# Attention by head pairs in a two-block transformer kernel: sum and maximum in one VectorE instruction, the causal mask as a matmul, projections cut in halves around the scores, finished rows fetched from another queue

## The chip, the cores and the metric

The kernel runs on one core of a Trainium2 chip. The time is the device time of one launch in microseconds. Three runs of the kernel before gave a median of 3226.95 us (3218.61 to 3236.28). The granted clock of TensorE is written as a share of its full speed.

## What is computed

Two model blocks follow each other on 1024 tokens of width 1024, all in float32. Each holds mixers between a wide input projection and an output projection. Three of the mixers are softmax attention, and they are what the change touches or borders on:

```python
# sparse attention (dsa): 6 heads of 64; each query sees its 256 best keys, with a bias by distance
logits = einsum('bqhd,bqkhd->bhqk', qb, kg) * (dh ** -0.5)
logits = logits + moveaxis(bias, -1, 1)          # rb[t5_bucket(rel)]; beyond some 128 tokens it is rb[31]
p = softmax(where(rel >= 0, logits, -1e30))
# forgetting attention (fox): 16 heads of 64, causal, c = cumsum(log_sigmoid(f))
s = einsum('bqhd,bkhd->bhqk', qi, k) * scale
s = s + ci[..., None] - ck[:, :, None, :]
pr = softmax(where(kpos <= qpos, s, -inf))
# dilated window attention (dil): 8 heads of 128 in three patterns
```

A softmax does not change when a number is added to a whole row. The term `ci` and the far bias `rb[31]` are such numbers.

## The kernel before

**Split products.** Every wide projection is made of three fp32r matmuls per 128x128 weight tile, high part by high, high by low, low by high (lines 820 to 822). A half projection, the unit in which the program is ordered, is one 128-column weight block by 512 tokens: 8 times 3 matmuls of 128x512 into one PSUM bank (`half_T`). `half_X` is a half too, but only four transposes, of the projected values. GpSimd splits each weight block into its two parts (lines 693 and 695), SyncE loads it.

**Stages of the kernel.** After norm, first projections and the key selection come 3 passes of sparse attention (500 to 710 us of the span), the output projection, 8 passes of forgetting attention (884 to 1584), output and gate, 8 passes of dilated attention (to about 3000), output, gate and final norm.

**A pass of pair attention** (`pair_attention`, on each engine) treats two heads of 64 at once, in 8 steps of 128 queries; step i sees (i+1)*128 keys, in chunks of at most 512, so that steps 4 to 7 have two chunks. VectorE adds the decay (fox) or the selection mask and the far bias (dsa) to the scores in PSUM (lines 2188 and 2192), adds the causal block or the near bias (line 2206), and takes the negated row maximum (line 2211), each for both heads. ScalarE takes the exponential in place (line 1723). TensorE transposes the probabilities (line 1106), ScalarE copies them back (line 1733), TensorE multiplies them with the values (line 1121) and spreads the reciprocals (line 1132). `sread`, `mx`, `edone`, `tdone`, `te` are the semaphores between them. VectorE and ScalarE run one step ahead of TensorE.

**The order on TensorE in a step** is written out by hand: transposes of chunk 0, spread of the step before, then `part1` of the next pair's projection, second score chunk of step i+1, values of chunk 0, transposes of chunk 1, `part2`, values of chunk 1, first score chunk of step i+2. `proj_units` deals the 10 halves of "TTTTX" over the 8 fox steps: one each, but two in step 3 and two in step 7, and those of step 7 are the transposes. In the sparse passes `SPARSE_UNITS` gives a half to steps 0, 2, 4, 6 and 7 only. The last pass of each kind has no projection beside it, apart from the turning of the residual in the sparse one and the first output block in step 7.

**Finished rows.** What attention has made goes to DRAM (`y_scratch`), one 512 KB row block a pass. In the last pass ScalarE loads six of them back, and after step 1 a seventh (`load_rows`, line 1659), copies each to its high part (line 1665), and GpSimd makes the low part (line 700). In the dilated stage ScalarE also issues, ahead of these, the load of the 4 MB residual (line 1798).

Of the kernel before, what the change touches and what calls it, by code (L numbers as in the profile page):

```python
# [15 lines left out]
P = 128  # L16
# [12 lines left out]
TOPK = 256  # L29
IDX_H, IDX_D = 4, 32  # L30
# [109 lines left out]
ORDER = dict(dsa="TTTTX", fox="TTTTX", dil="TTTTTTTTXTXTX")  # L140
PAIR_ROLES = (("q", 0), ("k", 0), ("vT", 0), ("g", 0), ("v", 0))
# [64 lines left out]
SPARSE_UNITS = {0: 0, 2: 1, 4: 2, 6: 3, 7: 4}  # L206
# [25 lines left out]
def beside_pair(kind, p, t):  # L232

    if kind == "dsa":
        n = SPARSE_UNITS.get(t)
        return ([] if n is None else [((5 * p + n) // 2, (5 * p + n) % 2, None)]), []
    return proj_units(kind, t)


# [12 lines left out]
def host_constants():  # L252
# [5 lines left out]
    out["c_ones"] = np.ones((P, P), np.float32)  # L258
    out["c_diag"] = np.where(q >= np.arange(P)[None, :], 0.0, NEG).astype(np.float32)
# [32 lines left out]
def build(nc, a):  # L292
    ctx = ExitStack()
    with ctx:
# [90 lines left out]
        h_flat = hT[:, :, :].rearrange("p k t -> p (k t)")  # L385
        F = Area(h_flat, 0, KB * T)
# [73 lines left out]
        ccol = FX.take(16 * NT).rearrange("p (t h) -> p t h", h=16)  # L460
# [54 lines left out]
        SPLIT = sems("act_split", "in late hi lo")  # L515
# [20 lines left out]
        FC = sems("foxc", "x lsig cum sent t ev")  # L536
# [4 lines left out]
        dil_in = sem("dil_constants")  # L541

# [3 lines left out]
        def load_gain(eng, m):  # L546
# [7 lines left out]
        def _(sp):  # L554
# [79 lines left out]

            def up_and_gate(m):
                for j in range(4):
                    out_block(m, j)
# [179 lines left out]
        def _(pe):  # L817
# [245 lines left out]
            def pair_attention(kind, base, first):  # L1063
# [7 lines left out]
                def project(p, units):  # L1071
                    for b, half, _ in units:
# [4 lines left out]
                        else:  # L1077
                            half_T(n, c, n % 2, half)

                def one(p, turn_, follow):  # L1080
                    Q = sets[kind][set_of(kind, p)]

                    def scores(i, c):
# [3 lines left out]
                        wait_pass(pe, S["sread"], before + p, C, starts[i] + c)  # L1087
# [64 lines left out]
                    for i in range(NT):  # L1152
                        part1, part2 = beside_pair(kind, p, i)
# [3 lines left out]
                        if follow:  # L1157
                            project(next_pair(kind, p), part1)
# [1435 lines left out]
```

## Time and profile before

| | |
|---|---|
| runs | 3218.61, 3226.95, 3236.28 us |
| profiled execution | 3224.9 us, its span 3223.1 us |
| PE busy | 2927.1 us (91%) |
| DVE, ACT, POOL busy | 1326.9, 903.2, 1033.6 us |
| mean granted clock | 0.954 |
| chain that ended last | PE 77%, DVE 13%, ACT 5% |

The profile names engines PE (TensorE), PEld (its weight loads), DVE (VectorE), ACT (ScalarE), POOL (GpSimd), SP (SyncE). In a timeline row a bracket gives the idle time before the instruction and what ended it. A row of the waits gives the engine and line that waited, what it waited for, the total in us, how often, and the longest.

### The profile page before, as it was taken

The page shows a single profiled execution, that of the slowest core. Times are in us where ns is not written, and L with a number is a line of the kernel's source. Part 1 is how long each engine was busy: PE and PEld are TensorE (multiplying, and loading weights), DVE is VectorE, ACT ScalarE, POOL GpSimd, SP SyncE. Part 2 cuts the span into 40 slices and gives each one's busy share as a digit, 9 for nine tenths or more (in the row PEclk, how much of TensorE's full clock was granted, in tenths as well). Part 3 has the DMA queues.
Part 4 walks back from the last instruction along what each step waited for, and adds up shares of the span by engine and source line. Part 5 has one row for each costly group of instructions (what it writes and reads, how often), then busy time and mean ns, then how long its engine had stood idle before and what let it go on. Part 6 is the DMA issues. An engine that isn't in the chain of part 4 may idle for free.

```text
span 3223.1 us, 39797 instructions
## 1 busy us (share of the span) xinstructions
PE 2927.1 (91%) x16484; PEld 2229.9 (69%) x16484; DVE 1326.9 (41%) x2447; ACT 903.2 (28%) x1689; POOL 1033.6 (32%) x447
## 2 busy tenths in 40 slices
PE   6979887879899998898899899999999999997998
PEld 4746674557666666665688677777777777775786
DVE  7999986555544444444634301111111111113322
ACT  4322313352233333333311322222222222223112
POOL 2613371124221212122353233342232323242541
PEclk8979899989999999999899999999999999998999
DMA  4100021031111111111122111111111111113211
GB/s 98 33 20 27 20 62 51 9 105 41 47 40 46 46 40 40 46 40 44 59 68 72 48 44 40 40 40 40 40 45 34 46 40 40 40 40 125 59 46 59
DMA packets 222223, 154.96 MB, mean 48 GB/s; under 512 B 26278, under 2 KB 208972, under 8 KB 221916
## 3 DMA queue, kind: packets, MB, share of 16 engines
q1 hardware_dynamic: 206908, 107.34, 11.9%
q10 hardware_dynamic: 15136, 45.08, 3.8%
q8 instruction: 131, 2.15, 0.3%
q14 instruction: 48, 0.39, 0.0%
HBM read 132.93 MB, written 19.47 MB: 47 GB/s over the span
## 4 chain that ended last, share of the span: by engine, by line
PE 77%; DVE 13%; ACT 5%; issue 3%; POOL 1%; DMA 1%; ACTq 0%; DVEq 0%; POOLq 0%
PE proj L820 20%; PE proj L821 19%; PE proj L822 19%; ACT arena L1723 3%; PE score L1106 2%; PE score L1092 2%; DVE arena L2154 2%; DVE arena L2152 2%; DVE arena L2206 2%; PE out L1121 2%; PE score L1235 1%; PE out L1288 1%; DVE arena L2289 1%; DVE arena L2211 1%; PE score L1244 1%
## 5 line engine op out<-in xcount | busy, mean ns | idle before, releaser
L820 PE MATMUL proj<-act_hi,w_hi 128*128 128x512 f32 x2592 | 1052.8, 406 | 46.7 <-POOL w_lo L695 28.3
L821 PE MATMUL proj<-act_lo,w_hi 128*128 128x512 f32 x2592 | 1025.4, 396 | 0.0
L822 PE MATMUL proj<-act_hi,w_lo 128*128 128x512 f32 x2592 | 1024.3, 395 | 0.0
L693 POOL TENSOR_TENSOR w_hi<-w_raw,ones 128x1024 fp32r<-128x1024 f32 x181 | 432.3, 2388 | 1844.2 <-PE proj L822 1827.3
L820 PEld LDWEIGHTS proj<-act_hi,w_hi 128*128 128x128 f32 x2592 | 496.8, 192 | 177.0 <-issue 33.6
L822 PEld LDWEIGHTS proj<-act_hi,w_lo 128*128 128x128 f32 x2592 | 496.2, 191 | 107.9
L821 PEld LDWEIGHTS proj<-act_lo,w_hi 128*128 128x128 f32 x2592 | 497.6, 192 | 99.6 <-issue 0.2
L695 POOL TENSOR_TENSOR w_lo<-w_raw,w_hi 128x1024 fp32r<-128x1024 f32 x181 | 448.9, 2480 | 14.2
L1707 ACT ACTIVATE arena<-proj 128x512 f32<-128x512 f32 x236 | 175.3, 752 | 922.5 <-PE proj L822 898.9
L2342 DVE SCALAR_TENSOR_TENSOR arena<-out,arena 128x128 f32<-128x128 f32 x64 | 17.9, 288 | 610.4 <-PE out L1254 610.4
L2188 DVE SCALAR_TENSOR_TENSOR arena<-score,arena 128x512 f32<-128x512 f32 (+2 forms) x192 | 109.6, 613 | 344.7 <-PE score L1092 344.7
L1106 PE MATMUL score<-ident,arena 128*128 128x128 f32 x792 | 141.2, 307 | 65.4 <-ACT arena L1723 63.5
L1106 PEld LDWEIGHTS score<-ident,arena 128*128 128x128 f32 x792 | 92.8, 151 | 146.8 <-ACT arena L1723 132.4
L2289 DVE SCALAR_TENSOR_TENSOR arena<-arena,score 128x256 f32<-128x256 f32 (+1 forms) x192 | 76.6, 427 | 264.1 <-PE score L1235 210.4
L2152 DVE MAX8 arena<-arena 128x8 f32<-128x384 f32 (+5 forms) x192 | 171.6, 894 | 5.9
L1723 ACT ACTIVATE arena<-arena 128x256 f32<-128x256 f32 (+7 forms) x176 | 134.9, 769 | 128.2 <-DVE arena L2211 128.2
L2154 DVE MATCH_REPLACE8 arena<-arena 128x384 f32<-128x384 f32 (+5 forms) x192 | 168.5, 878 | 0.0
L1733 ACT ACTIVATE arena<-score 128x512 f32<-128x512 f32 (+3 forms) x264 | 119.4, 487 | 115.1 <-PE score L1106 113.1
L1707 ACT ACTIVATE hT<-proj 128x512 f32<-128x512 f32 x78 | 65.7, 850 | 273.2 <-PE proj L822 258.1
L1121 PE MATMUL out<-arena 128*64 128x128 f32 x1296 | 102.3, 295 | 29.4 <-ACT arena L1733 29.4
L2211 DVE TENSOR_REDUCE arena<-arena 128x1 f32<-128x256 f32 (+7 forms) x176 | 123.5, 742 | 0.0
L1121 PEld LDWEIGHTS out<-arena 128*64 128x64 f32 x1296 | 74.9, 145 | 65.8 <-ACT arena L1733 40.3
(244 smaller groups left out, 3058.1 us busy)
## 6 DMA issues: line engine op xcount, KB each, us to landing
w_raw<-dil_w_in_dram SPq DMA_DIRECT2D x80, 512.0 KB, 3.7
w_raw<-fox_w_in_dram SPq DMA_DIRECT2D x32, 512.0 KB, 4.0
w_raw<-w_in_dram SPq DMA_DIRECT2D x23, 512.0 KB, 3.8
y_scratch<-arena ACTq DMA_DIRECT2D x21, 512.0 KB, 3.7
act_lo<-y_scratch ACTq DMA_DIRECT2D x21, 512.0 KB, 8.1
arena<-decay_scratch ACTq DMA_DIRECT2D x16, 512.0 KB, 5.3
w_raw<-ple_w_gate_dram SPq DMA_DIRECT2D x16, 512.0 KB, 3.8
arena<-x_dram SPq DMA_DIRECT2D x12, 512.0 KB, 4.1
```

What stands on the lines that cost most here:

```text
L693: pool.tensor_tensor(hi, raw, one.unsqueeze(1).broadcast_to([P, KB, P]), ALU.mult).then_inc(w_hi_done, 1)
L695: pool.tensor_tensor(lo, raw, hi.bitcast(F32), ALU.subtract).then_inc(w_split, 1)
L820: pe.matmul(bank, hi, a_hi, start=first, stop=False)
L821: pe.matmul(bank, hi, a_lo, start=False, stop=False)
L822: return pe.matmul(bank, lo, a_hi, start=False, stop=last)
L1106: mm = pe.transpose(score[:, 1, hh * 512 + b * P:hh * 512 + (b + 1) * P], R["p"][hh][i % 2][:, (b0 + b) * P:(b0 + b + 1) * P], ident[:, :])
L1121: mm = pe.matmul(obanks[i % 2][cols, 0:P], Q["v"][0][:, b0 + b, cols], R["pT"][hh][:, q % 2, b * P:(b + 1) * P], start=(b0 + b == 0), stop ...
L1707: act.activation(dst, src, ACT.Copy, scale=scale if role == "q" else 1.0).then_inc(pass_free[half], 1)
L1723: act.activation(R["p"][hh][i % 2][:, 0:width], R["p"][hh][i % 2][:, 0:width], ACT.Exp, bias=R["st"][:, s:s + 1], accum_out=R["st"][:, 16 ...
L2152: dve.max(top8, scores[:, 0:w]).then_inc(IX["top"], 1)
L2154: dve.match_replace(scores[:, 0:w], top8, scores[:, 0:w], -3e38).then_inc(IX["top"], 1)
L2211: dve.tensor_reduce(R["st"][:, s:s + 1], R["p"][hh][i % 2][:, 0:width], AX.X, ALU.max, negate=True)\
```

## The change

1. VectorE: in fox a single instruction (`tensor_tensor_reduce`) adds decay and scores, negates, and keeps a running minimum; the per-query decay `ccol`, its transposes and its copy are gone, and so are the block add and the maximum. In dsa the far part of a row is made by the same instruction, the last 256 columns by a plain add out of PSUM and then one such instruction with the bias table; `rb31` is gone. The exponential gets `scale=-1.0`.
2. TensorE: in fox the last 128 columns of a row get the causal block by a bf16 matmul of identity and block, one per head, accumulated on the scores. `diag` is reloaded for it as packed bf16.
3. `pair_units` replaces `proj_units` and `SPARSE_UNITS`; "TTTTX" becomes "TTTXT". In fox each step has one full half, cut in two parts of 12 matmuls, of which the first stands ahead of the second score chunk and the second after the transposes of chunk 1. In the sparse passes each step has one such part.
4. SyncE loads the finished rows, in `up_and_gate` and beside the residual loads, ahead of the weights that follow, and the 4 MB residual after them. ScalarE waits per two rows (`in0`, `in1`, `in2`).

```diff
-ORDER = dict(dsa="TTTTX", fox="TTTTX", dil="TTTTTTTTXTXTX")
+ORDER = dict(dsa="TTTXT", fox="TTTXT", dil="TTTTTTTTXTXTX")
+PAIR_HALVES = ((0, 0), (0, 1), (1, 0), (1, 1), (2, 0), (2, 1), (3, 0), (4, 0), (3, 1), (4, 1))
+def pair_units(kind, p, t):
+    def unit(n, part=None):
+        return (n // 2, n % 2, part)
+    if kind == "fox":
+        n = t if t < 6 else t + 2
+        return ([unit(7)] if t == 6 else []), unit(n, 0), unit(n, 1), ([unit(6)] if t == 5 else [])
+    if p == 0:
+        return [], unit(t // 2, t % 2), None, []
+    n = 4 + t // 2 if t < 4 else 6 + t // 2
+    return ([unit(7)] if t == 4 else []), unit(n, t % 2), None, ([unit(6)] if t == 3 else [])
...
+        def scores_read(eng, kind, p, q):
+            S, before = AT[kind], PAIRS_BEFORE[kind]
+            chunks = chunks_of(attention_steps(kind))
+            starts = chunk_starts(chunks)
+            if kind == "dsa":
+                wait_pass(eng, S["sread"], before + p, starts[-1], q)
+                return
+            i = max([0] + [i for i in range(NT) if starts[i + 1] <= q])
+            if q == 0 or starts[i + 1] == q:
+                eng.wait_ge(S["mx"], 2 * NT * (before + p) + (2 * (i + 1) if q else 0))
+            else:
+                partial = [q_ for q_ in range(1, q + 1) if q_ not in starts]
+                eng.wait_ge(fox_read, p * (starts[-1] - NT) + len(partial))
...
+            def finished_rows(kind, base):
+                m = MIXER[kind]
+                for half in range(2):
+                    sp.wait_ge(pass_done[half], base + PASSES[kind] * len(ORDER[kind]))
+                sp.wait_ge(AT[kind]["ysent"], 16 * (STORES_BEFORE[kind] + PASSES[kind] - 2))
+                for j, k in enumerate(rows_before(m)[:6]):
+                    sp.dma_start(act_lo[:, k].bitcast(F32), yd[k * P:(k + 1) * P, :]).then_inc(SPLIT[f"in{j // 2}"], 16)
+            def late_row(kind):
+                k = rows_before(MIXER[kind])[6]
+                sp.wait_ge(AT[kind]["ysent"], 16 * (STORES_BEFORE[kind] + PASSES[kind] - 1))
+                sp.dma_start(act_lo[:, k].bitcast(F32), yd[k * P:(k + 1) * P, :]).then_inc(SPLIT["late"], 16)
...
+                if m == 1:
+                    finished_rows("fox", C_FOX)
+                    late_row("fox")
+                else:
+                    finished_rows("dil", C_DIL)
+                    late_row("dil")
+                    sp.wait_ge(AT["dil"]["sdone"], 2 * NT * (PASSES["dil"] - 1) + 1)
+                    sp.dma_start(hT[:, :, :], xd).then_inc(xback, 16)
...
+            sp.wait_ge(IX["sel"], 9)
+            sp.dma_start(diag[:, :].bitcast(I32), a["c_diag_half"]).then_inc(halved, 16)
...
+                    if t == 2:
+                        sp.wait_ge(GL["ysent"], 16 * 5)
+                        finished_rows("dsa", C_DSA)
+                        late_row("dsa")
                     sp.wait_ge(N0["raw"], 2 * (t - 2) + 2)
...
                             mm = pe.matmul(score[:, 0, hh * 512:hh * 512 + w], Q["q"][0][rows, i * P:(i + 1) * P],
-                                           Q["k"][0][rows, lo:lo + w], start=True, stop=True)
+                                           Q["k"][0][rows, lo:lo + w], start=True, stop=not causal(i, lo, w),
+                                           skip_group_check=causal(i, lo, w))
+                        if causal(i, lo, w):
+                            for hh in range(2):
+                                end = hh * 512 + w
+                                mm = pe.matmul(score[:, 0, end - P:end], diag_half[:, 0], diag_half[:, 1], start=False, stop=True,
+                                               skip_group_check=True)
                         mm.then_inc(S["sdone"], 1)
...
-                            act.activation(R["p"][hh][i % 2][:, 0:width], R["p"][hh][i % 2][:, 0:width], ACT.Exp,
-                                           bias=R["st"][:, s:s + 1], accum_out=R["st"][:, 16 + s:17 + s]).then_inc(S["edone"], 1)
+                            act.activation(R["p"][hh][i % 2][:, 0:width], R["p"][hh][i % 2][:, 0:width], ACT.Exp,
+                                           bias=R["st"][:, s:s + 1], scale=-1.0, accum_out=R["st"][:, 16 + s:17 + s]).then_inc(S["edone"], 1)
...
-                    if not follow:
-                        load_rows(kind, True, base)
...
+                                if kind == "fox":
+                                    ins = dve.tensor_tensor_reduce(row[:, lo:lo + w], cB[turn_][hh][:, lo:lo + w], src, -1.0,
+                                                                   most if c else LARGE, ALU.add, ALU.min, most)
+                                at = mask_offset(i) + lo
+                                if far:
+                                    ins = dve.tensor_tensor_reduce(row[:, lo:lo + far], maskb[:, at:at + far], src[:, 0:far], -1.0,
+                                                                   most if c else LARGE, ALU.add, ALU.min, most)
+                                if far < w:
+                                    ins = dve.tensor_tensor(row[:, lo + far:lo + w], src[:, far:w], maskb[:, at + far:at + w], ALU.add)
+                        if kind == "dsa":
+                                dve.tensor_tensor_reduce(row[:, near:width], row[:, near:width], tbias[:, 2 * p + hh, 2 * P - width + near:2 * P],
+                                                         -1.0, most if near else LARGE, ALU.add, ALU.min, most).then_inc(S["mx"], 1)
-                            dve.tensor_tensor(row[:, width - w:width], row[:, width - w:width], near, ALU.add)\
-                               .then_inc(S["pre"], 1)
-                            dve.tensor_reduce(R["st"][:, s:s + 1], R["p"][hh][i % 2][:, 0:width], AX.X, ALU.max, negate=True)\
-                               .then_inc(S["mx"], 1)
```

## Rows read from the trace of the kernel before

**Rows 1.** By stage: length, busy PE, PEld, DVE, ACT, POOL, then granted clock, DMA.
```profile
500.00:647.00 147.00, 124.26 (x788) 82.02 (x786) 76.56 (x157) 54.93 (x124) 18.92 (x8) 0.93 0.05 19
647.00:710.00 63.00, 47.83 (x331) 30.96 (x330) 44.70 (x95) 37.40 (x78) 16.70 (x7) 0.86 0.38 134
884.00:1519.00 635.00, 578.68 (x3434) 407.89 (x3436) 276.28 (x565) 210.02 (x467) 136.67 (x57) 0.96 0.14 41
1519.00:1584.00 65.00, 50.21 (x332) 30.70 (x329) 41.95 (x95) 31.19 (x65) 16.50 (x7) 0.81 0.18 65
```
**Rows 2.** Waits of PE in the fox passes 0 to 6 (884 to 1519).
```profile
PE score L1106 <- ACT arena L1723: 36.6, 37, 3.3
PE out L1121 <- ACT arena L1733: 12.9, 27, 0.6
PE score L1092 <- DVE arena L2188: 5.7, 7, 0.8
```
**Rows 3.** Waits of PE in sparse passes 0 and 1 (500 to 647).
```profile
PE score L1106 <- ACT arena L1723: 16.4, 18, 3.5
PE score L1092 <- DVE arena L2192: 10.4, 4, 9.2
PE out L1121 <- ACT arena L1733: 4.7, 8, 0.7
```
**Rows 4.** Timeline of a fox pass around its step 7.
```profile
1142.61 1.41 DVE L2188 SCALAR_TENSOR_TENSOR arena<-score,arena 128x512 f32<-128x512 f32 x2 [7.22 <-PE score L1092]
...
1144.03 2.35 POOL L695 TENSOR_TENSOR w_lo<-w_raw,w_hi 128x1024 fp32r<-128x1024 f32 x1
1144.05 2.67 DVE L2206 TENSOR_TENSOR arena<-arena,diag 128x128 f32<-128x128 f32 x2
...
1146.65 2.33 DVE L2211 TENSOR_REDUCE arena<-arena 128x1 f32<-128x1024 f32 x2
1147.89 1.15 ACT L1723 ACTIVATE arena<-arena 128x1024 f32<-128x1024 f32 x1 [2.91 <-DVE arena L2211]
...
1149.18 2.25 PE L1106 MATMUL score<-ident,arena 128*128 128x128 f32 x8 [3.27 <-ACT arena L1723]
```
**Rows 5.** Timeline of PE at a change between projection and attention, and eight transposes.
```profile
1064.15 1.09 PE L1106 MATMUL score<-ident,arena 128*128 128x128 f32 x8
...
1075.40 0.39 PE L822 MATMUL proj<-act_hi,w_lo 128*128 128x512 f32 x1
1075.71 0.44 PE L1121 MATMUL out<-arena 128*64 128x128 f32 x4
...
1078.18 0.50 PE L820 MATMUL proj<-act_hi,w_hi 128*128 128x512 f32 x1
1078.52 0.40 PE L821 MATMUL proj<-act_lo,w_hi 128*128 128x512 f32 x1
1078.76 0.39 PE L822 MATMUL proj<-act_hi,w_lo 128*128 128x512 f32 x1
```
**Rows 6.** Timeline of the last fox pass: row loads, then values.
```profile
1526.21 3.56 ACTq L1659 DMA_DIRECT2D act_lo<-y_scratch  x6
...
1531.32 0.70 PE L1121 MATMUL out<-arena 128*64 128x128 f32 x4 [5.35 <-ACT arena L1733]
```
**Rows 7.** Timeline of the last dilated pass.
```profile
2946.41 1.08 PE L1288 MATMUL out<-arena 128*32 128x128 f32 x16 [4.50 <-ACT arena L1790]
...
2961.89 2.00 ACT L1665 ACTIVATE act_hi<-act_lo 128x1024 fp32r<-128x1024 f32 x2 [9.87 <-DMA act_lo<-y_scratch]
...
2964.43 1.08 PE L1288 MATMUL out<-arena 128*32 128x128 f32 x16 [6.79 <-ACT arena L1790]
```
**Rows 8.** VectorE's groups of instructions, whole span.
```profile
L2154 DVE MATCH_VALUE_LOAD arena<-arena 128x8 f32 x192 | 17.7, 92 | 6.6
L2251 DVE SCALAR_TENSOR_TENSOR arena<-arena 128x1024 f32<-128x1024 f32 x9 | 11.0, 1227 | 12.5 <-ACT arena L1752 12.4
L2045 DVE TENSOR_TENSOR_SCAN arena<-arena 128x1024 f32<-128x1024 f32 x2 | 6.1, 3093 | 0.0
```

More of the change, by code:

```diff
@@ L1 @@
 from contextlib import ExitStack
+from itertools import product
 import math
@@ L205, with units_done @@
 RESIDUAL_TURNS = ((0,), (1,), (2,), (3,), (4,), (5,), (6, 7), ())
-SPARSE_UNITS = {0: 0, 2: 1, 4: 2, 6: 3, 7: 4}
+PAIR_HALVES = ((0, 0), (0, 1), (1, 0), (1, 1), (2, 0), (2, 1), (3, 0), (4, 0), (3, 1), (4, 1))
[9 more added lines that the diff above has]
+    return ([unit(7)] if t == 4 else []), unit(n, t % 2), None, ([unit(6)] if t == 3 else [])
+def units_done(units):
+    return [u for u in units if u is not None and u[2] != 0]
 def pass_beside(n):
@@ L258, in host_constants @@
     out["c_ones"] = np.ones((P, P), np.float32)
+    halves = np.concatenate([np.eye(P, dtype=np.float32), np.where(q >= np.arange(P)[None, :], 0.0, NEG).astype(np.float32)], axis=1)
+    out["c_diag_half"] = np.ascontiguousarray(halves.view(np.uint32) >> 16).astype(np.uint16).view(np.int32)
     out["c_diag"] = np.where(q >= np.arange(P)[None, :], 0.0, NEG).astype(np.float32)
@@ L1071, in project @@
                 def project(p, units):
-                    for b, half, _ in units:
+                    for b, half, part in units:
                         n = p * NW + base + weight_of(order, b)
@@ L1077, in project, with causal @@
                         else:
-                            half_T(n, c, n % 2, half)
+                            half_T(n, c, n % 2, half, part)
+                def causal(i, lo, w):
+                    return kind == "fox" and lo + w == (i + 1) * P
                 def one(p, turn_, follow):
@@ L1086, in scores @@
                             return
[L1087 removed]
+                        scores_read(pe, kind, p, starts[i] + c)
                         lo = 512 * c
@@ L1176, in one @@
                         scores(i + 2, 0)
+                        if follow:
+                            project(next_pair(kind, p), tail)
                     if not follow:
                         spread(NT - 1)
-                halves = [(b, half, None) for b in range(NB) for half in range(2)]
+                halves = [(b, half, None) for b, half in PAIR_HALVES]
                 if kind == "dsa":
@@ L1342, in attention @@
                 out_last(m, kind)
-            def forget_columns():
-                pe.wait_ge(FC["cum"], 1)
-                for t in range(NT):
-                    mm = pe.transpose(obank[:, t * 16:t * 16 + 16], crow[0:16, t * P:(t + 1) * P], ident[0:16, 0:16])
-                mm.then_inc(FC["t"], 1)
-                pe.wait_ge(FC["ev"], 1)
-                later(pe, NF, "back", 2 * KB)
             def turn_p(m, b):
@@ L1649, in _ @@
                 gla_step(n)
-            def load_rows(kind, first, base):
-                m = MIXER[kind]
-                if kind == "dsa" and first:
-                    act.wait_ge(GL["ysent"], 16 * 5)
-                act.wait_ge(AT[kind]["ysent"], 16 * (STORES_BEFORE[kind] + PASSES[kind] - (2 if first else 1)))
-                for half in range(2):
-                    act.wait_ge(pass_done[half], base + PASSES[kind] * len(ORDER[kind]))
-                for k in rows_before(m)[:6] if first else rows_before(m)[6:]:
-                    act.dma_start(act_lo[:, k].bitcast(F32), yd[k * P:(k + 1) * P, :]).then_inc(SPLIT["in" if first else "late"], 16)
             def split_rows(m, i):
@@ L1826, in attention @@
                         projected(0, 0, [(0, half, None), (1, half, None)])
-                halves = [(b, half, None) for b in range(NB) for half in range(2)]
+                halves = [(b, half, None) for b, half in (PAIR_HALVES if kind != "dil" else product(range(NB), range(2)))]
                 if kind == "dsa":
```

85 lines of the change are left out of this document (37 added, 48 removed).

## The prediction

> **What bounds the kernel now.** I read the page first: PE is busy for 91% of the span and makes 77% of the chain that ended last. So an edit pays where PE stands still or runs at a low clock, or where it takes work off PE; what it takes off VectorE (41% busy) pays only through that. The table by stage then says where PE stands still [rows 1]. The fox passes 0 to 6 last 635 us with PE busy 578.7, at a mean clock of 0.96; the last fox pass has 14.8 us without PE in 65; the sparse passes have 22.7 in 147 and, the last, 15.2 in 63. Everything else in the kernel is outside the change, but for the last dilated pass. The waits say for whom PE stood: in fox 55.2 us (36.6 + 12.9 + 5.7), nearly all for the exponential or for ScalarE's copy [rows 2]. In the two sparse passes it is 31.5 us, of which one wait of 9.2 us is the end of the key selection, which the change leaves: 22.3 us are in play [rows 3]. The timeline of step 7 shows what stands behind "waits for the exponential" [rows 4]: scores are read by two adds in 1.41 us, then come the block adds (2.67 us for two of 128 columns, while GpSimd's product runs, longer than two of 512 columns out of PSUM), the two maxima (2.33 us), and the exponential begins 5.3 us after the first add. PE has only transposed values as cover there and waits 3.27 us. After that wait the eight transposes take 2.25 us, against 1.09 us elsewhere [rows 5]; part of that is the second head's wait, part the clock. Of the two levels, 1.2 and 2.4 GHz, a mean of 0.96 over 635 us is 51 us at the lower one.
>
> **VectorE, fox.** Removed per step: two block adds and two maxima; the adds stay as the new instruction. In step 7 the exponential could start after one add and its accumulation, some 0.8 us after the scores, in place of 5.3. No row has the new instruction. Below: the same time as the old one, 0.70 us for 512 columns [rows 4]. Above: the rate of the running scan, 3093 ns for 1024 columns [rows 8], which is 1.5 us for 512. I take the old time plus 0.1 us, as the small second instruction that match-replace brings costs 92 ns [rows 8], since one source and one result are as before. VectorE is not on the path of the fox passes at either end: between the second score chunk and the next read of PE on the same bank lie 5.8 us of PE work (values 1.1, transposes 0.9, the second part of the half 2.9, values 0.9).
>
> **The cuts, fox.** Each step now has a full half, and half of it lies between the score chunk and the transposes that wait for it. Chunk-1 scores to the exponentials' end is then 0.1 + 1.6 + 2.6, about 4.3 us, beside 5.8 of PE work plus the next scores. ScalarE has the copy of chunk 1 (1.1 us) ahead of the exponential in its queue, and it still fits. What stays is the start of a pass, where the scores of step 1 wait for row 0 and nothing covers it: 1.5 to 2 us a pass. So of 55.2 us 14 stay and **41 go**. The long waits being gone, I give back **14 us of clock**, from nothing to 25 (half of the 51).
>
> **What PE gets in return.** The mask: 8 steps of 8 passes with 2 matmuls, 128 in all. Nearest row: eight float32 transposes of 128 columns in 1.09 us, 7 steps of 0.117 us [rows 5]. 128 by 0.117 is **15 us lost**; below 0, should they hide in the gaps; above, unpipelined, the 0.27 us of one transpose and 0.14 of its weight load, 52 us. The cuts: within a half the starts follow each other by 0.24 us (1078.52 to 1078.76); on leaving it the next start comes after 0.31 (1075.40 to 1075.71), on coming back the second comes after 0.34 (1078.18 to 1078.52) [rows 5]; 0.2 us a cut, 56 cuts in fox and 8 in the sparse passes, **13 us lost**, from nothing to 0.5 us each, 32. The transposes of `ccol` and the wait for their copy save 1 us.
>
> A rule of the Trainium skill puts the mask lower: TensorE: Matmul & The Clock Gate, section Back-to-back issue gap, gives 134 cycles for 128 columns, which would be 7 us for the 128. No run here shows a bf16 matmul in a stream, and the sum does not use it.
>
> **The last fox pass.** ScalarE issues six loads, 3.56 us on its queue, ahead of the gate and the first copy, and PE waits 5.35 us for that copy [rows 6]. With SyncE issuing them the gate's 1.1 us and the copy stay: 3.8 us gained. In the six later steps the exponential now waits for ScalarE's own copy of chunk 1 rather than the maximum, so a step gains some 1 us, not the whole block add and maximum: 6 us. Two adds no longer collide with GpSimd: 2 us. Together **12**.
>
> **The sparse passes.** The far part is covered as in fox, but the last 256 columns need a plain add and a second pass, so a wide row gets only some 0.8 us shorter; the collision with GpSimd stays, since both sources of the bias instruction are in SBUF. What helps is that each step has a part as cover, in place of five steps in eight. ScalarE's queue (copy, then exponential) leaves some 1.2 us a wide step, 5 us a pass. 22.3 less 10 is **12**, with **3 of clock**. The last pass gains the same 3.8 from the row loads and some 4 from the rows: **8**. There SyncE has seven row loads ahead of the residual's third tile; that tile is needed two steps into the pass, so I price it at nothing; if its cover fails, it is one load, 4 us, in one step.
>
> **The last dilated pass.** PE waits 4.50 us for the copy behind ScalarE's issues and 6.79 us behind ScalarE's wait of 9.87 us for a row that lands after the 4 MB residual [rows 7]. SyncE starts the rows when the projections end, ahead of the pass's first exponential, and puts the residual behind them; the copies to the high parts (2.0 us) move forward. **10 of 11.3**. VectorE wants the residual only after the pass, so it is late for nobody. SyncE's weight loads behind these waits are split by GpSimd only after the seven rows, so they hide too.
>
> **Sum.** 41 + 14 + 1 + 12 + 12 + 3 + 8 + 10 = 101 gained, 15 + 13 = 28 lost, 73 us net. Against the profiled execution, 3224.9 us (its span 3223.1), that is 3152; the median of the runs shown lies 2 us above it, so 3154 us.
>
> **Rivals.**
> 1. *The waits only move.* ScalarE's queue or the score bank ends the step in place of VectorE. For it: ScalarE has copies, exponentials and evacuation in a fixed order. Against: it is busy for 210 us in 635 [rows 1]. If half of the fox and sparse gains (41, 12, 14, 3) stay away, 35 us, the time is 3189. Chance 0.17.
> 2. *The clock stays up and mask and cuts hide.* 11 more of clock, 28 not lost: 3115. Chance 0.1.
> 3. *Slower: the new instruction has a large fixed cost.* Four passes lack cover to take it: the three sparse ones with 32 each and the last fox one with 24, 120 in all, of which two thirds are on the path. At f us each this is 80 f, and it eats the 73 us at f of 0.9; past 1.1 it is slower by 0.5%. At 1.5 us it is 3274. The one small second instruction among its rows takes 92 ns [rows 8]. Chance 0.04.
> 4. *Two float32 sources in SBUF at half the rate.* For the 48 bias instructions of the sparse passes: 256 columns, 0.27 us each, 13 us on VectorE, 9 on the path: 3163. The row against: two sources in SBUF, 1024 columns in 1227 ns [rows 8], full rate, but without accumulation. Chance 0.12. This is a point of the Trainium skill, Vector Engine (DVE) Microarchitecture Reference, section Points that are easy to get wrong, which says that such an instruction halves its throughput because no port is left for the accumulator; by that rule, the row of the plain instruction disagrees, and whether the new one follows it no run here shows.
> 5. *The change does not do what it says*: the mask's unpipelined price, 37 us more, takes back what the cover brings: 3191. Chance 0.05.
>
> **How the numbers follow.** The forecast itself has 0.52, with an own range of 3135 to 3173. The range reaches up to rivals 1 and 5 and down to rival 2: 3115 to 3192, leaving out rival 3 and tails, some 0.18. This kernel's measurement tells some 0.5%, 16 us, from no change; faster by more is all below 3211, so all but rival 3 and the tail of 1 and 5. Faster 0.92, within 0.5% 0.04, slower 0.04.
>
> **What would show it.** In the new profile a fox pass should last some 86 us instead of 90.7 (635 by 7), PE's waits for the exponential there fall to a fifth, the clock of the stage rise to 0.98 or more; the new VectorE instruction should take some 0.7 us in the mean, a mask matmul add 0.1 us to a step; no wait over 2 us should stand behind ScalarE at the start of the three last passes. I am wrong if new waits of PE stand at the scores behind VectorE, if the new instruction takes over 1.5 us for 512 columns, or if PE's busy time in fox rises by more than 35 us.

## The result and the profile after

| | before | after |
|---|---|---|
| median (runs) | 3225.99 us (3218.61 to 3236.28, 4) | 3126.37 us (3119.94 to 3129.75, 4) |
| profiled execution, span | 3224.9, 3223.1 us | 3124.53, 3122.7 us |
| PE, DVE, ACT, POOL busy | 2927.1, 1326.9, 903.2, 1033.6 us | 2899.4, 1137.8, 895.2, 1031.9 us |
| granted clock | 0.954 | 0.966 |

The ratio is 0.9679, with a 95% interval of 0.9660 to 0.9698: the changed kernel is faster by some 100 us. The forecast was 3154 us, inside a range of 3115 to 3192, and 73 us of gain.

The windows of the changed kernel, cut where its stages begin and end, answer to [rows 1]: sparse passes 0 and 1, the last sparse pass, fox passes 0 to 6, the last fox pass, and the last dilated pass.

```profile
502.00:632.00 130.00, 117.20 (x788) 78.41 (x788) 57.79 (x213) 52.89 (x124) 18.20 (x8) 0.97 0.09 30
632.00:678.00 46.00, 39.66 (x316) 25.38 (x313) 31.74 (x117) 34.59 (x75) 15.06 (x7) 0.96 0.47 161
856.00:1438.00 582.00, 570.61 (x3582) 399.72 (x3582) 131.65 (x509) 207.77 (x470) 132.99 (x57) 0.99 0.15 43
1438.00:1478.00 40.00, 33.19 (x272) 19.28 (x270) 21.40 (x83) 27.99 (x61) 17.82 (x8) 0.96 0.40 131
2844.00:2894.00 50.00, 32.72 (x378) 21.53 (x367) 30.40 (x68) 19.60 (x35) 15.79 (x7) 0.83 0.50 186
```

In fox, VectorE's busy time has halved (276.28 us [rows 1], now 131.65) and PE stands still for 11 us in 582.

For the difference to close, each stage is cut at an instruction that both kernels have (an attention stage begins with its first score matmul, the sparse one with the scores of its step 1, and a last pass ends at the first matmul of the output projection in its step 7) and its length is split in three from the trace: time in which PE has no matmul; time in which it works while the record of the granted clock stands at the lower level, of which half is lost, since that level is half the other; and the rest, its work at full clock. All in us, "idle" and "low" being the first two:

| stage | before: length, idle, low | after: length, idle, low | gained |
|---|---|---|---|
| sparse passes 0, 1 | 146.9, 22.7, 20.1 | 129.2, 12.3, 6.6 | 17.7 |
| last sparse pass | 59.6, 15.2, 11.9 | 46.7, 6.3, 3.4 | 12.9 |
| fox passes 0 to 6 | 639.4, 56.8, 44.6 | 582.1, 11.4, 6.8 | 57.3 |
| last fox pass | 53.9, 14.5, 17.6 | 40.2, 6.8, 3.4 | 13.7 |
| dilated passes 0 to 6 | 1018.2, 39.8, 6.1 | 1025.4, 40.6, 19.8 | -7.2 |
| last dilated pass | 58.0, 24.2, 15.9 | 50.0, 17.3, 14.0 | 8.0 |
| all else | 1247.1, 122.8, 105.6 | 1249.1, 128.6, 97.2 | -2.0 |
| sum | 3223.1, 296.0, 221.8 | 3122.7, 223.3, 151.2 | 100.4 |

So 72.7 us came from idle time, 35.3 from the clock (half of 70.6), and 7.6 were paid in work, which is what is left of the 100.4. The 7 us lost in the dilated passes are the lower level, in code that the change does not touch: its share there lay anywhere between 6 and 24 us over the kernels run below, and at 6.3 in e8, which has all of the change. Of the 2 us in "all else", 3 are real, at the start (last section).

The waits of PE, fox passes 0 to 6, answer to [rows 2]:

```profile
PE score L1158 <- DVE arena L2240: 5.8, 7, 1.1
PE out L1193 <- ACT arena L1790: 5.6, 6, 1.7
PE score L1158 <- ACT arena L1764: 0.9, 1, 0.9
```

55.2 us have become 12.3. No wait for an exponential is left; every wait that stays lies within the first 10 us or so of a pass. In the sparse passes, answering to [rows 3], the 9.1 us are the end of the key selection again:

```profile
PE score L1158 <- DVE arena L2252: 9.7, 2, 9.1
PE score L1178 <- ACT arena L1780: 7.0, 8, 1.8
PE out L1193 <- ACT arena L1790: 4.7, 8, 0.7
```

The timeline of a fox pass around step 7 answers to [rows 4] (the rows of weight loads and projections are left out):

```profile
1338.38 1.13 PE L1158 MATMUL score<-arena 64*128 64x512 f32 x4
1339.44 0.29 PE L1164 MATMUL score<-diag 128*128 128x128 bf16 x2
1339.65 1.10 PE L1193 MATMUL out<-arena 128*64 128x128 f32 x16
1339.76 0.75 DVE L2240 CUSTOM_DVE_ANT_0 arena<-arena,score 128x512 f32<-128x512 f32 x1 [5.03 <-PE score L1164]
1340.43 0.08 DVE L2240 DVE_READ_ACCUMULATOR2_ANT arena<- 128x1 f32 x1
...
1341.27 0.87 ACT L1790 ACTIVATE arena<-score 128x384 f32<-128x384 f32 x2 [4.94 <-PE score L1178]
...
1342.02 1.15 ACT L1780 ACTIVATE arena<-arena 128x1024 f32<-128x1024 f32 x1
...
1345.03 1.09 PE L1178 MATMUL score<-ident,arena 128*128 128x128 f32 x8
```

The new instruction shows as two, the sum and the read of its accumulator. After 0.8 us the first head is ready; the exponential starts 2.3 us after the first sum, no longer held by VectorE but by ScalarE's own copy. The transposes follow with no wait and take 1.09 us. VectorE's groups by form:

```profile
L2240 DVE CUSTOM_DVE_ANT_0 arena<-arena,score 128x512 f32<-128x512 f32 x96 | 63.2, 696 | 225.0 <-PE score L1158 140.0 <-PE score L1164 85.0
L2260 DVE CUSTOM_DVE_ANT_0 arena<-arena 128x256 f32<-128x256 f32 x42 | 28.6, 718 | 0.7
L2240 DVE DVE_READ_ACCUMULATOR2_ANT arena<- 128x1 f32 x192 | 15.8, 83 | 0.0
L2240 DVE CUSTOM_DVE_ANT_0 arena<-arena,score 128x256 f32<-128x256 f32 x32 | 13.1, 447 | 28.7 <-PE score L1164 28.7
```

The starts of the last fox and last dilated pass answer to [rows 6, 7]:

```profile
1436.94 2.75 SPq L674 DMA_DIRECT2D act_lo<-y_scratch  x6
...
1443.12 0.44 PE L1193 MATMUL out<-arena 128*64 128x128 f32 x4 [2.21 <-ACT arena L1790]
```

```profile
2842.22 2.80 SPq L674 DMA_DIRECT2D act_lo<-y_scratch  x6
...
2850.58 0.79 PE L1364 MATMUL out<-arena 128*32 128x128 f32 x16
...
2854.91 1.99 ACT L1722 ACTIVATE act_hi<-act_lo 128x1024 fp32r<-128x1024 f32 x2
...
2855.38 0.32 SPq L680 DMA_DIRECT2D act_lo<-y_scratch  x1
2855.47 0.29 DVE L2391 SCALAR_TENSOR_TENSOR act_hi<-out,arena 128x128 fp32r<-128x128 f32 x1 [0.85 <-DMA y_scratch<-arena]
...
2855.75 0.43 SPq L692 DMA_DIRECT2D hT<-x_scratch  x1
2856.03 4.70 POOL L763 TENSOR_TENSOR act_lo<-act_lo,act_hi 128x1024 fp32r<-128x1024 f32 x2 [10.35 <-ACT act_hi L1722]
2856.06 2.47 DVE L2397 TENSOR_TENSOR act_lo<-arena,act_hi 128x128 fp32r<-128x128 f32 x1
...
2859.10 1.22 PE L1320 MATMUL score<-arena 128*128 128x256 f32 x2 [3.33 <-DVE arena L2340]
```

The six issues stand on SyncE. In fox the wait of 5.35 us is 2.21, in the dilated pass those of 4.50 and 6.79 us are gone. But there a new one has come: since the copies to the high parts are made earlier, GpSimd's products of the same rows now meet a small subtraction of VectorE (line 2397), which takes 2.47 us here, and PE waits 3.33 us for the scores that VectorE reads behind it. Its six instructions in this stage took 3.7 us before (one of them 2.19) and take 7.5 now. PE's waits for VectorE's additions to the scores, which stand in the same queue, first before (2936 to 2994), then after (2844 to 2894):

```profile
PE score L1244 <- DVE arena L2289: 7.9, 6, 3.0
```

```profile
PE score L1320 <- DVE arena L2340: 12.3, 6, 3.3
```

With the loads back on ScalarE (e7 below) they are 8.9 us.

### The profile page after: what moved, and what is told of

It is laid out like the page before. It is cut to its first block, busy times and chain, and to the rows that moved or that the text cites. A ratio compares the mean times of both kernels' runs of the same rounds, so it can differ in the third digit from the quotient of the medians.

```text
span 3122.7 us, 40092 instructions
## 1 busy us (share of the span) xinstructions
PE 2899.4 (93%) x16604; PEld 2208.9 (71%) x16604; DVE 1137.8 (36%) x2460; ACT 895.2 (29%) x1689; POOL 1031.9 (33%) x447
## 4 chain that ended last, share of the span: by engine, by line
PE 82%; DVE 9%; issue 3%; ACT 3%; DMA 1%; POOL 1%; ACTq 1%; DVEq 0%; POOLq 0%
PE proj L883 20%; PE proj L884 19%; PE proj L885 19%; PE score L1158 3%; PE out L1193 3%; PE score L1178 3%; DVE arena L2202 2%; DVE arena L2200 2%; PE score L1311 2%; DVE arena L2340 1%; PE out L1364 1%; PE score L1320 1%; PE out L1369 1%; PE out L1204 1%; PE out L883 1%
## 5 line engine op out<-in xcount | busy, mean ns | idle before, releaser
L2240 DVE CUSTOM_DVE_ANT_0 arena<-arena,score 128x512 f32<-128x512 f32 (+2 forms) x192 | 102.8, 572 | 428.2 <-PE score L1164 288.0
L1178 PE MATMUL score<-ident,arena 128*128 128x128 f32 x792 | 117.7, 283 | 9.6 <-ACT arena L1780 9.3
L1178 PEld LDWEIGHTS score<-ident,arena 128*128 128x128 f32 x792 | 85.2, 141 | 55.4 <-issue 30.0
L1158 PE MATMUL score<-arena 64*128 64x512 f32 (+3 forms) x432 | 99.8, 539 | 9.7 <-DVE arena L2240 7.3
L1193 PE MATMUL out<-arena 128*64 128x128 f32 x1296 | 95.9, 282 | 11.8 <-ACT arena L1790 11.8
L883 PE MATMUL proj<-res_parts,w_hi 128*128 128x512 f32 x256 | 101.5, 397 | 0.0
```

Of the source, the lines that this page charges most:

```text
L883: pe.matmul(bank, hi, a_hi, start=first, stop=False)
L1178: mm = pe.transpose(score[:, 1, hh * 512 + b * P:hh * 512 + (b + 1) * P], R["p"][hh][i % 2][:, (b0 + b) * P:(b0 + b + 1) * P], ident[:, :])
L1193: mm = pe.matmul(obanks[i % 2][cols, 0:P], Q["v"][0][:, b0 + b, cols], R["pT"][hh][:, q % 2, b * P:(b + 1) * P], start=(b0 + b == 0), stop ...
```

## The experiments

Runs sent together share a chip and the runs of the kernel before. Below, "changed" is the changed kernel, 3126.37 us (ratio 0.9679). The same kernel on another chip took 3122.95 us (e12, below), so differences of some 3 us between runs that were not sent together say nothing in the total; the stages of the trace are steadier (fox passes 0 to 6 last 582 us in both).

**What the mask costs.** The first run has no mask matmuls, so its rows are not causal; the second has three for each.

```diff
-                    return kind == "fox" and lo + w == (i + 1) * P
+                    return kind == "fox" and lo + w == (i + 1) * P and False
```

> The changed kernel without the 128 mask matmuls in the forgetting passes; it leaves out the causal block of a row, all else is as it was. If the price is the one of the forecast (0.117 us each, all of it on TensorE's path), it is 15 us faster than the changed kernel, 3111 us. If a mask matmul costs half of that, as a rival from the stage sum would have it (the stage shows mask and cuts together at some 9 us, where 24 were priced), it is 7 us faster, 3119 us. If the masks hide in waits, the time stays at 3126 us, and the waits of TensorE for VectorE and ScalarE in the stage (12 us) rise by what is taken away.

```diff
-                                mm = pe.matmul(score[:, 0, end - P:end], diag_half[:, 0], diag_half[:, 1], start=False, stop=True,
-                                               skip_group_check=True)
+                                for again in range(3):
+                                    mm = pe.matmul(score[:, 0, end - P:end], diag_half[:, 0], diag_half[:, 1], start=False, stop=again == 2,
+                                                   skip_group_check=True)
```

> The changed kernel with each mask matmul issued three times, 256 more of them; the mask only becomes more negative. Same theories, other side and twice the lever: 0.117 us each gives 30 us more, 3156 us; half of it 15 us more, 3141 us; hidden: 3126 us. If the three matmuls of one bank stand 0.06 us apart in the timeline, the stream price is the lower one and the rest is the price of the change of weights.

Measured: 3111.46 us (ratio 0.9643, 0.9622 to 0.9663) and 3140.5 us (0.9733, 0.9712 to 0.9755), 15 us less and 14 more than changed. Clock and idle time left aside, the work at full clock in the whole span is 10.9 us less and 13.7 more: 0.085 us for each of 128 and 0.054 for each of 256 further ones. The timelines agree. In the changed kernel a pair takes 0.21 us of PE's time (1339.44 to 1339.65 above); with three of each:

```profile
1401.18 0.34 PEld L1165 LDWEIGHTS score<-diag 128*128 128x128 bf16 x6
1401.18 0.51 PE L1165 MATMUL score<-diag 128*128 128x128 bf16 x6
1401.62 1.10 PE L1194 MATMUL out<-arena 128*64 128x128 f32 x16
```

0.44 us for six, so 0.23 for the four added. The forecast's 0.117 was too much, and a third (by the work) to a half (by the timeline) of what a mask matmul costs belongs to the change from float32 scores to the mask, not to the stream. The expectation of e1 (3111 us at 0.117 each) was met by its total, but 4 of its 15 us are clock and idle time.

The Trainium skill (TensorE: Matmul & The Clock Gate, section Back-to-back issue gap) has 134 cycles for 128 columns, 0.056 us at 2.4 GHz, as the gap of an isolated matmul. The same section of the Trainium skill puts the spacing in a stream of weight loads and matmuls at some 81 ns for 128 columns. The trace agrees with the first, though each of the six matmuls has a weight load of its own: 0.057 us.

**Where the half projection stands.** Both runs have 56 cuts fewer. The diff is that of the first (e3), the half ahead of the second score chunk; the second (e4) has `None, unit(n)` there, the half behind the transposes of chunk 1.

```diff
-        return ([unit(7)] if t == 6 else []), unit(n, 0), unit(n, 1), ([unit(6)] if t == 5 else [])
+        return ([unit(7)] if t == 6 else []), unit(n), None, ([unit(6)] if t == 5 else [])
```

> The changed kernel with the half projection of a fox step in one piece, ahead of the second score chunk (56 cuts gone, the second place empty). If a cut costs the forecast's 0.2 us and nothing needs its cover, it is 11 us faster, 3115 us. Main theory: the cover is needed. From the second score chunk to the transposes that wait for its exponential only values, transposes, values and the next scores are left, some 4.0 us of PE work against the 4.3 us of chain (scores read 1.6, exponentials 2.6), and the exponential stands behind a copy: 0.5 to 1 us of wait in four steps of each of seven passes, 14 to 28 us, so 3130 to 3145 us, with TensorE waiting for the exponential at the transposes in steps 4 to 7.

> The changed kernel with the half of a fox step in one piece behind the transposes of chunk 1 (56 cuts gone, the first place empty). If only the long cover matters (second score chunk to the next transposes), it is 11 us faster, 3115 us. Main theory: the values of chunk 0 then follow the transposes they need with nothing between but the spread in the steps without a second score chunk (0, 1, 2 and 7): ScalarE's copy takes some 1.4 us from the transposes' end, so about 1 us of wait in 28 steps, 28 us less the 11 us of cuts, 3143 us, with the waits standing at the values behind the copy.

Measured: 3139.65 us (0.9728, 0.9706 to 0.9751) and 3156.48 us (0.9779, 0.9756 to 0.9801). Fox passes 0 to 6 lasted 595.3 and 613.8 us in place of 582.1. PE's waits there, first with the half in the first place, then in the second:

```profile
PE out L1193 <- ACT arena L1790: 16.3, 28, 0.7
PE score L1158 <- DVE arena L2240: 5.8, 7, 1.1
PE score L1178 <- ACT arena L1780: 5.0, 14, 0.5
```

```profile
PE out L1193 <- ACT arena L1790: 27.3, 28, 3.7
PE score L1158 <- DVE arena L2240: 6.2, 8, 1.1
```

The sum of the first was right and its reason was not: most of the wait (16.3 us, 28 times) stands at the values, for ScalarE's copy, and only 5.0 at the exponential. For the second it is the other way round: 28 waits of a mean 1 us are as expected, but the sum (3143) was 13 us too low, since the lower clock came back with the waits (6.8 us at the lower level to 38.4, worth 15.8) and no term stood for it. So the cut halves serve two covers, one for the exponential and one for each copy.

**Each part alone.** e5 and e9 are the changed kernel with the old order; in e5 the order of the dilated heads was altered by mistake ("TTTTTTTTTXXTX"), so that only its sparse and fox stages count. e6 is the kernel before with the new order alone.

```diff
-ORDER = dict(dsa="TTTXT", fox="TTTXT", dil="TTTTTTTTXTXTX")
+ORDER = dict(dsa="TTTTX", fox="TTTTX", dil="TTTTTTTTXTXTX")
+SPARSE_UNITS = {0: 0, 2: 1, 4: 2, 6: 3, 7: 4}
+    part1, part2 = proj_units(kind, t)
```

> The changed kernel without its third part: the order TTTTX, whole halves, two of them in steps 3 and 7 of a forgetting pass, and a half in five of the eight sparse steps, as before; the new VectorE instruction, the mask matmuls and SyncE's row loads stay. Main theory, that order and shorter rows both were needed: the whole half ahead of the second score chunk cost 13 us, step 7 has only transposes as cover again (some 3 us in 7 passes), the sparse passes lose some 5, so 3126 + 13 + 20 + 5, some 3160 us with a clock again lower at the ends of the passes. Rival, that the VectorE part alone brought the gain: 3135 to 3145 us.

> The kernel before with the third part alone: order TTTXT, halves cut in two around the second score chunk, a part in each sparse step. VectorE's adds, block adds and maxima, its ccol and ScalarE's row loads are those of before. Main theory: the new place of the halves gives 7.8 us of cover behind the second score chunk, against a chain of 5.3 us to the exponential and 2.3 of exponentials, so that most of the 57 us without TensorE in the seven passes goes, but not all in steps in which GpSimd's product holds up the block add: some 30 us of wait and 10 of clock are gained, cuts cost 6, 3190 us. Rival: the row in VectorE is still too long, nothing is gained and the cuts cost: 3225 to 3235 us. Other rival: order alone does all of it: 3150 us.

> The changed kernel without its third part, once more, now with the order of the dilated heads as it is in both kernels (the run before had it altered). From the stages of that run: 10 us more than the changed kernel in the seven forgetting passes, 2.6 in the sparse ones, 1 in the last passes, and 3 less ahead of them: 3137 us. That is the gain of 89 us from the VectorE part, the mask and the row loads without the order. Rival, that the altered dilated order had hidden a loss elsewhere: 3150 us or more.

| fox passes 0 to 6 | total | length | idle | low | work |
|---|---|---|---|---|---|
| before | 3225.99 | 639.4 | 56.8 | 44.6 | 560.2 |
| e6, order alone | 3167.92 | 572.5 | 8.2 | 9.9 | 559.3 |
| e9, all but the order | 3131.53 | 590.5 | 24.1 | 0.0 | 566.5 |
| changed | 3126.37 | 582.1 | 11.4 | 6.8 | 567.2 |
| e11, below | 3105.28 | 568.9 | 7.8 | 3.0 | 559.5 |

e6 has a ratio of 0.9806 (0.9768 to 0.9844), e9 of 0.9713 (0.9687 to 0.9739); e5 was 3122.9 us, with 592.2 us in the fox passes. Alone, the order gains 56 us against the runs of the kernel before that were sent with it (63 by the ratio) and the other three parts some 91, together 100: they take away the same waits. The total of e9 does not stand clear of that of the changed kernel (3131.53 against 3126.37, intervals that overlap); its stages do, with 8.4 us more in fox passes 0 to 6 and 2.5 in the sparse passes. All three expectations missed on the same side: e5's 3160 and e6's 3190 assumed that both parts were needed. In fox passes 0 to 6 the order alone, with VectorE's long rows, is 9.6 us *faster* than the whole change, by 7.9 us of work, which is mostly the mask (without the mask matmuls the changed kernel has 557.9 in e1, 559.5 in e11). And e11, which has the order and the new instruction without the mask matmuls, is only 3.6 us better there than the order alone: once each step has its cover, the shorter rows are worth little in these passes. Where the cover is smaller they are worth more: with ScalarE's loads in both, sparse passes 0 and 1 last 147.5 us in e6 and 129.1 in e7 (below), the last fox pass 52.5 and 44.6. In the sparse stages it is the rows that count and not the order: passes 0 and 1 last 146.9 us before, 147.5 with the order alone, 131.7 in e9, 129.2 in the changed kernel.

**The row loads.** ScalarE issues them (and the residual) again.

```diff
+                    if not follow:
+                        load_rows(kind, True, base)
...
-                    finished_rows("fox", C_FOX)
-                    late_row("fox")
```

> The changed kernel without its fourth part: ScalarE issues the row loads again (and the 4 MB residual in the dilated pass), SyncE does not. By the forecast it costs 3.8 us in the last sparse and 3.8 in the last forgetting pass and 10 in the last dilated one, 17.6 us and no clock: 3144 us. The stages of the changed kernel show 8.9, 7.7 and 6.9 us less without TensorE in these three passes and some 6 us of clock. If all of that belongs to the loads, it is 3156 us; if the shorter rows did the work and the loads hide, 3130 us.

Measured: 3142.6 us (0.9737, 0.9709 to 0.9765), 16 us more. The last sparse pass is 6.2 us longer, the last fox pass 4.4, the last dilated pass 5.0, together 15.6. The forecast of 17.6 was near.

**How much room VectorE has.**

```diff
+                                    dve.tensor_tensor(row[:, lo:lo + w], cB[turn_][hh][:, lo:lo + w], src, ALU.add).then_inc(twice, 1)
+                                    wait_pass(dve, twice, p, 2 * C, 2 * (starts[i] + c) + hh + 1)
```

> The changed kernel with a plain add of the same operands and shape ahead of each new VectorE instruction of the forgetting passes, and a wait for it: VectorE's time for a row doubles, some 13 us more in each of the eight passes, TensorE's work is as it was. Main theory, VectorE has slack of 1.5 us in a step that has a half as cover, and none at the start of a pass and in the last pass: 1 us in each of seven passes and some 9 in the last, 3142 us, with hardly a wait for the exponential in the middle of a pass. Rival, that VectorE's chain still sets the pace: two thirds of 8 times 13 us, 3195 us.

Measured: 3134.45 us (0.9716, 0.9687 to 0.9746). Fox passes 0 to 6 are 5.1 us longer, the last one 10.5 (6.6 of them idle, 4.2 clock). Seven waits for VectorE at the starts of passes (5.8 us, now 9.4) are all that is new in the middle passes:

```profile
PE score L1159 <- DVE arena L2243: 9.4, 7, 1.3
PE out L1194 <- ACT arena L1791: 6.0, 5, 2.0
PE score L1159 <- ACT arena L1765: 0.9, 1, 0.9
```

**The mask back on VectorE.** If VectorE has room and PE has none, the mask belongs to VectorE. e10 does so in passes 0 to 6, e11 in all eight, e12 is the changed kernel again, on the chip of e11.

```diff
+                                    if far < w:
+                                        ins = dve.tensor_tensor(row[:, lo + far:lo + w], src[:, far:w], cB[turn_][hh][:, lo + far:lo + w], ALU.add)
...
+                                dve.tensor_tensor_reduce(row[:, near:width], row[:, near:width], diag_half[:, 1],
+                                                         -1.0, most if near else LARGE, ALU.add, ALU.min, most).then_inc(S["mx"], 1)
```

> The changed kernel with the causal block added by VectorE in the seven forgetting passes that have projections beside them: the last 128 columns of a row by a plain add, then one new instruction with the block (bf16) as second source, as the sparse passes do it; the last pass keeps the mask matmuls. 112 of 128 mask matmuls go, at 0.085 us each 9.5 us. Main theory, VectorE has room there (with the order alone and the old, longer rows the seven passes lasted 572.5 us, against 582.1 in the changed kernel, with less time without TensorE): 3117 us, faster than the changed kernel. Rival: the block instruction has both sources in SBUF and stands beside GpSimd's products, and waits come back at the starts of passes and in single steps, 1 us or more a pass: 3126 us or above.

> As the run before (causal block by VectorE), now in the last forgetting pass too, so that no mask matmul is left. There TensorE has no projection as cover. TensorE loses 16 mask matmuls, 1.4 us; VectorE has two more instructions and an accumulator read for each head and step, 0.29 + 0.50 + 0.08 us less the 0.13 that the first instruction gets shorter, 0.74 us, 1.5 us a step, 12 us in the pass. The doubled adds put 10.5 us of some 13 on the path there. Main theory: the last pass is 7 to 9 us longer (40.6 to some 48), 3118 us. Rival, VectorE has room there too: 1 us shorter, 3109 us.

> The changed kernel again, beside the runs with the mask on VectorE, to compare them on one chip: 3126 us, 8 us slower than the run with all blocks on VectorE if the last pass loses 7 to 9 us there; its fox passes 0 to 6 last 582 us and those of the other 568.

Measured: e10 3110.74 us (0.9638, 0.9613 to 0.9664), e11 3105.28 us (0.9624, 0.9607 to 0.9641), e12 3122.95 us (0.9679, 0.9661 to 0.9698). On one chip e11 is 17.7 us faster than the changed kernel, and no run of the one reaches into the runs of the other (3103.96 to 3107.15, 3119.85 to 3128.56). Both are faster than their forecasts (3117 and 3118). In fox passes 0 to 6 the work falls by 7.7 us and the idle time by 3.6; with the last pass the stages that the edit touches give 11.5 us. The other 6 stand in the dilated passes, in code that both kernels share, and vary there from kernel to kernel as said above: that they come from the mask is not shown. The windows of e10 for these passes, against 570.61 us of busy PE in 582:

```profile
863.00:1431.00 568.00, 559.68 (x3468) 392.13 (x3468) 187.76 (x789) 210.36 (x471) 134.48 (x57) 1.00 0.15 44
```

VectorE is busy 56 us more, and PE waits for it no longer than in the changed kernel (seven times at the starts of passes, 4.8 us against 5.8). The last pass, where I had put 7 to 9 us, was 1.7 us longer than in e12 (42.0 against 40.3): its waits for the exponential are 2.0 us where they were 0.7.

## Why the prediction was right

The direction, the bound and the mechanism (long waits for the exponential go, and with them the time at the lower clock) held. The total came nearer than its terms did. The 27 us that the forecast lacked are made of three errors: costs booked at 28 us were 7.6 (20 too high), the clock booked at 17 gave 35.3 (18 too low), and waits booked at 84 gave 72.7 (11 too high), which the first two hide. In the last passes the clock had no term at all. And one attribution was wrong. By its own terms:

- **Waits in fox**, 41 of 55.2, 14 to stay: 42.9 went and 12.3 stayed, at the starts of passes as forecast (1.7 us a pass).
- **Clock in fox**, 14: 18.9 (half of 44.6 less 6.8). The bound of 25 was right; half of it was too cautious. In the record of the clock before, a stretch at the lower level begins at every end of a pass, as at 1148.2 us, where the wait of 3.27 us in [rows 4] falls, nine from 885 to 1514; after, two are left, at 857.5 and 1195.5 us, and in e4 they were back, seven of them, with the waits.
- **Mask**, 15 for 128: 10.9. The term was mis-sized by the nearest row: a transpose's 0.117 us for a stream that costs 0.054 and an entry that costs the rest.
- **Cuts**, 13 for 64: too high, and no single price came out. Without them the fox work is 4.1 us less in e3 and 8.6 in e4, 0.07 to 0.15 us a cut; but e6 has all the cuts and no more work than before (559.3 against 560.2), and e9 has none and saves 0.7. At most 0.15, perhaps nothing; which, stays open. Mask and cuts were booked at 28 us; the work of the span grew by 7.6.
- **ccol**, 1: not seen; the stage ahead of fox took 177.1 us and takes 177.4.
- **Last fox pass**, 12 less 2 of mask: 13.7, but by luck: 7.7 of it is idle time and 7.1 is clock, which was not booked. The loads are 4.4 of it (3.8 forecast), by e7.
- **Sparse passes 0 and 1**, 12 and 3 of clock: 10.4 of idle time and 6.8 of clock. The size held, the reason failed: "what helps is that each step has a part as cover". e6 has that cover and gains nothing there, e9 has not and gains 15.2 of 17.7: the shorter rows did it.
- **Last sparse pass**, 8: 12.9, of which 8.9 are idle time and 4.3 the clock. The loads are 6.2 of it, by e7.
- **Last dilated pass**, 10: 8.0, of which 6.9 are idle time. What failed there is a wait that had no term: the 11.3 us behind ScalarE are gone, but 4.4 have come back behind VectorE, by the subtraction that now meets GpSimd's products. With the loads back on ScalarE the stage is 55.0 us, 3.0 short of the 58.0 before; that ScalarE now waits for two rows at a time may be the reason, which was not run by itself, and with SyncE's loads the stage itself lay anywhere between 47.7 and 50.6 us.
- **The new instruction**, 0.8 us for 512 columns: 0.696 and 0.083.

**The rivals.** The waits did not merely move (1), apart from the 4.4 us in the last dilated pass. The clock stayed up (2), and its 3115 us was nearer than 3154 to what came, though mask and cuts did not hide: e1 and e2 show the masks paid in full. A fixed cost of the new instruction (3) is 0.083 us. Two float32 sources in SBUF at half rate (4): the bias instruction has a mean of 718 ns for 256 columns against 447 with a source in PSUM, which looks like the rule, 0.27 us more. But of all 48 bias instructions, 41 took 0.29 to 0.49 us, one 0.59, and six took 1.7 to 2.6; one of these six, in the timeline of the last sparse pass:

```profile
646.93 2.54 POOL L763 TENSOR_TENSOR act_lo<-act_lo,act_hi 128x1024 fp32r<-128x1024 f32 x1
647.19 2.57 DVE L2260 CUSTOM_DVE_ANT_0 arena<-arena 128x256 f32<-128x256 f32 x1
```

It is as long as GpSimd's product beside it. The seven that took more than 0.5 us are those that met such a product, so the mean comes from few collisions, not from a rate. The point of the Trainium skill (Vector Engine (DVE) Microarchitecture Reference, section Points that are easy to get wrong) is made there for another instruction, `S2S2D2_STT`. In this one it did not show: 0.48 us for 256 columns alone. Rival 5 is excluded by e1 and e2.

**The signs.** A fox pass lasts 83.1 us (86 forecast), the clock of the stage is 0.99, the new instruction takes 0.70 us. One sign failed: a wait of 2.21 us, over the 2 us allowed, still stands behind ScalarE at the start of the last fox pass.

What the prediction did not ask is whether each part was needed beside the others. It summed over one list of waits and gave all of it to the change as a whole, which is why the total held while the parts overlapped by half. The shorter rows, without the mask and the loads, were not run alone, so their share of e9's 91 us is open.

## What to carry to other kernels

Two edits that remove the same waits are not worth their sum; run each alone, since the second may keep only its cost. Here the mask matmul moved work from an engine with room (VectorE, whose rows could be doubled for 5 us in seven passes) to the one that sets the end, and moving it back gave 11.5 us more in the forgetting passes. Moving work forward can put it beside something new: the last dilated pass gave back 4.4 of 11.3 us in that way. Cover has to be placed for every wait in the step, the short ones behind a copy as well as the long one behind the exponential; a half projection cut in two did more than a whole one in either place.

## What the runs showed of the hardware

- A 128-column bf16 matmul onto float32 sums costs 0.054 us in a row of its like, each with its weight load, and a pair of them between float32 matmuls 0.21 us.
- An instruction of VectorE with both float32 sources in SBUF is held up by a GpSimd product that it meets (2.57 us beside 2.54, against 0.48 alone). All seven bias instructions of 256 columns that met one ended 0.28 us after the product's end, whenever they had begun. The 49 sums of 512 columns out of PSUM that met one took 0.69 us in the mean and at most 0.75, the 45 that did not 0.70 and at most 0.75.
- Changing the place of the value transposes among the halves cost 3 us far away, ahead of the first sparse pass: time without PE from the start to the first score rose from 72.8 us to 76.3 and in e6 to 76.0, and is 73.2 in e9. ScalarE issues six loads of the bias table (2.74 us) ahead of its copy of the transposed values. Before, no copy that PE waited for came behind these loads; in the changed kernel one does:

```profile
469.87 2.74 ACTq L1688 DMA_DIRECT2D arena<-bias_scratch  x6
...
472.66 0.60 ACT L1764 ACTIVATE hT<-proj 128x512 f32<-128x512 f32 x1 [2.20 <-issue]
473.40 0.47 PE L883 MATMUL proj<-act_hi,w_hi 128*128 128x512 f32 x1 [3.14 <-ACT hT L1764]
```
